# A hybrid-attention and mixture-of-experts encoder block on one core: early loads dealt to two queues, one warm-up pair of products less, and an earlier turn of the second query tile

## The chip, the cores and the metric

The kernel runs on one core of one Trainium2 chip. The metric is the device time of one execution in microseconds (us), with all weights and inputs in the chip's DRAM at the start. Three timed runs of the kernel before gave 576.99, 577.24 and 577.96 us: the median is 577.24 us.

## The reference, cut to what matters

One encoder layer over 256 tokens of width 1024, everything in float32:

```python
n = rms_norm(h, norm1_g)
p = n @ w_in                      # 1024 x 1536: columns [qA | kA | vA | qB | kB | vB]
A = global attention, 8 query heads, 2 key/value heads; q and k are RMS-normalised per head and rotated
B = windowed attention (|i-j| <= 128), 8 heads, sink logit per head, T5 relative-position bias
h = h + concat[rms_norm(A), rms_norm(B)] @ w_o
h = h + hier_moe(rms_norm(h, norm2_g))   # top-1 of 4 groups, then top-2 of its 8 experts
return rms_norm(h, final_g)

# hier_moe: 32 experts, each silu(x @ w_gate) * (x @ w_up) @ w_down
#           w_gate, w_up: 1024 x 512; w_down: 512 x 1024 (2 MB each, so 6 MB an expert)
```

The 32 experts have 201 MB of weights; all of them are read once.

## The kernel before

All of it is one program written engine by engine, with semaphores between the engines: SyncE (`sp`) issues nearly all loads in a fixed order, ScalarE (`act`) issues a few, TensorE (`pe`), VectorE (`dve`) and GpSimd (`pool`) compute. Each engine works through its own list in the order in which it is written, and a wait stops everything behind it on that engine. Tokens are two tiles of 128 (t = 0, 1).

**Start (lines 300 to 320, 483 to 500, 656 to 661, 1011 to 1052).** SyncE loads the gains `gT` (12 KB), then in turn the four pieces of the transposed input `xT` (256 KB each, two column chunks a piece) and the eight chunks of `w_in` (768 KB each), the input itself (`h`, two halves) after chunk 5, and two tables of constants. ScalarE at the same time issues seven small loads: `onehot` (32 partitions of 2 KB), `relb` (32 partitions of 32 bytes), and five that spread a row over 128 partitions (`qn_g`, `kn_g`, `sink`, `b_group`, `b_expert`). TensorE multiplies zeros twice (`multiply_zeros(2)`, two products of 128x128 by 128x512, each of which shows as two passes), waits for `onehot` and `relb`, makes with them one product of 32x8 by 32x512, the line of the relative-position bias (line 1018), and multiplies zeros twice more. VectorE scales each chunk of `xT` by `gT`. Then TensorE projects: for each of the 8 chunks c it waits for the scaled `xT` chunk and for `w_in` chunk c and makes three products (line 1032); after these come eight products more that need nothing new. ScalarE copies the bias line out of PSUM (line 493), GpSimd masks it, ScalarE stores it to DRAM and, once `w_in` chunk 5 has landed, reads it back in shifted rows (`bias_in`), after which SyncE goes on with `w_o` and the experts' weights.

**Attention (lines 1055 to 1160).** Eight steps s = 0 to 7, each of four heads: `scores`, the row maxima (`maxima`, VectorE), the exponentials (`exps`, ScalarE), `turn_probs` (transposes), the cut of these (`cut_probs`, one half on VectorE, one on ScalarE) and `weigh_v`. Steps 0 to 3 are the windowed group, 4 to 7 the global one. In between VectorE rotates the global queries of each tile (`rotate(t)`, with GpSimd's help for the norm), TensorE turns them (`turn(ps[7], pair_cols(t, ...))`) and VectorE copies them (`turn_out`), which steps 4, 5 (tile 0) and 6, 7 (tile 1) need. Scores of step s + 2 are issued at the end of step s. Also in between TensorE projects the mixed heads by `w_o` (`project`, line 1101, bank 7), and VectorE adds that to `h` (`add_projection`, line 727).

**Experts (from line 1201).** A ring of 11 slots of 2 MB holds weights. `sp` issues the load of fill f once fill f - 11 has been used (`wait_used`). Units 0 to 3 have 2 experts, the seven behind them 4; a unit gathers its tokens, multiplies by gate and up (line 1240), by down (line 1255), and scatters (line 1277).

Of the kernel before, what the change touches and what calls it, by code (L numbers as in the profile page):

```python
# [116 lines left out]
def build_encoder(nc, x, x_cols, gain_cols, norm1_g, w_in, qn_g, kn_g, sink, rel_bias, gnorm_a, gnorm_b, w_o, norm2_g,  # L117
# [10 lines left out]
    with ExitStack() as ctx:  # L128
# [171 lines left out]

        @block.sync
        def _(sp):
            sp.dma_start(gT[:], gain_cols).then_inc(gain_in, 16)
            for c in range(KC):
                if c < 4:
                    sp.dma_start(xT[:, 2 * c:2 * c + 2, :], x_cols[:, 2 * c:2 * c + 2, :]).then_inc(xT_in[c], 16)
                sp.dma_start(w_in_sb[:, c, :], w_in_c[c]).then_inc(w_in_in[c], 16)
                if c == 5:
                    for t, arrived in enumerate((x_in, x1_in)):
                        sp.dma_start(h[:, t, :], x_t[t]).then_inc(arrived, 16)  # L310
            sp.dma_start(cst[:], consts).then_inc(consts_in, 16)
# [168 lines left out]

        @block.scalar
        def _(act):
            act.dma_start(onehot_sb, onehot).then_inc(onehot_in, 16)
            act.dma_start(relb_sb, rel_bias).then_inc(onehot_in, 16)
            act.dma_start(gains[:, 0, :], qn_g[0].partition_broadcast(P)).then_inc(small_in, 16)
            act.dma_start(gains[:, 1, :], kn_g[0].partition_broadcast(P)).then_inc(small_in, 16)
            act.dma_start(sink_b[:], sink[0].partition_broadcast(P)).then_inc(router_in, 16)
            act.dma_start(router_b[:, 0:4], b_group[0].partition_broadcast(P)).then_inc(router_in, 16)
            act.dma_start(router_b[:, 4:36], b_expert[0].partition_broadcast(P)).then_inc(router_in, 16)


            act.wait_ge(line_ready, 1)
            act.activation(line_sb, ps[7][0:8, :], ACT.Copy).then_inc(line_cut, 1)
            act.wait_ge(line_masked, 1)
            act.dma_start(bias_line, line_sb).then_inc(line_stored, 16)
            act.wait_ge(line_stored, 16)
            act.wait_ge(w_in_in[5], 16)
            shifted = bass.AP(bias_line.tensor, 0, [[1, P], [4 * P, 8], [1, 3 * P]])
# [148 lines left out]
        def _(dve):  # L647
# [68 lines left out]
            def mix_out(g, t, k, bank=7):  # L716

                dve.wait_ge(mix_turned, k)
                dve.tensor_tensor(mixT[:, 1 - g, t], ps[bank][:].rearrange("p (c t) -> p c t", c=4),
                                  bcast(gT[:, 8 + 4 * g:12 + 4 * g], 2, P), ALU.mult).then_inc(mixT_ready, 1)  # L720
# [29 lines left out]
                dve.tensor_tensor(qt_, qt_, bcast(rq[t], 2, HD), ALU.mult).then_inc(roped, 1)  # L750

            for s in range(8):
                if s != 3:
                    maxima(s)
                if s >= 1:
                    cut_probs(s - 1)
                if s == 0:
                    dve.wait_ge(qk_turned, 4)
                    dve.tensor_copy(qkT[:, 4, :], ps[5][:, 256:512]).then_inc(qkT_ready, 1)
                if s == 2:  # L760
                    maxima(3)
                    dve.wait_ge(qkv_done, 4)
                if s >= 2:
                    outputs(s - 2)
                if s == 1:
                    rotate(0)
                if s == 2:
                    turn_out(5, 0)
                if s == 3:
                    mix_out(1, 0, 1)  # L770
                    rotate(1)
                if s == 4:
                    dve.wait_ge(ro_ready, 1)
                    add_projection(1, 0, 0, 1, 7)
                    turn_out(6, 1)
                if s == 5:
                    add_projection(1, 0, 1, 2, 7)
                if s == 6:
                    mix_out(1, 1, 2)
                if s == 7:  # L780
                    dve.wait_ge(ro_ready, 2)
                    add_projection(1, 1, 0, 3, 7)

                    dve.wait_ge(router_w_in, 32)
                    dve.tensor_tensor(router_w, router_w, bcast(gT[:, 16:24], 2, 36), ALU.mult).then_inc(router_ready, 1)
# [224 lines left out]
        def _(pe):  # L1010
            def multiply_zeros(n):
                for _ in range(n):
                    pe.matmul(ps[6][:], zeros[:, 0:P], zeros[:, P:P + 512], start=True, stop=True)  # L1013
# [2 lines left out]
            multiply_zeros(2)  # L1016
            pe.wait_ge(onehot_in, 32)
            pe.matmul(ps[7][0:8, :], relb_sb, onehot_sb, start=True, stop=True).then_inc(line_ready, 1)
            multiply_zeros(2)

            def turn(dst, srcs, done):

                for k, src in enumerate(srcs):
                    last = pe.transpose(dst[:, k * P:k * P + src.shape[0]], src, ident[0:src.shape[0], 0:src.shape[0]])
                last.then_inc(done, 1)
# [69 lines left out]
            def turn_mix(g, t, bank):  # L1095
                pe.wait_ge(o_ready, 4 * (1 - g) + 2 * t + 2)
                turn(ps[bank], [o_sb[:, t, 512 * g + c * P:512 * g + (c + 1) * P] for c in range(4)], mix_turned)
# [21 lines left out]
            for s in range(8):  # L1119
# [4 lines left out]
                    turn(ps[7], [pair_cols(0, b) for b in range(0, 4)], qk_turned)  # L1124
                if s == 3:
                    turn_mix(1, 0, 7)
                if s >= 1:
                    weigh_v(s - 1)
                if s == 2:
                    pe.wait_ge(qkT_ready, 5)  # L1130
                if s == 4:
                    pe.wait_ge(roped, 2)
                    pe.wait_ge(h_added, 1)
                    turn(ps[7], [pair_cols(1, b) for b in range(0, 4)], qk_turned)
                    pe.wait_ge(qkT_ready, 6)
                if s + 2 < 8:
                    scores(s + 2)
# [253 lines left out]
```

## Time and profile before

| | |
|---|---|
| Median of three runs | 577.24 us (576.99 to 577.96) |
| Profiled execution, whole | 579.82 us |
| Its span, first to last instruction | 578.0 us |
| TensorE busy | 442.7 us (77%) |
| VectorE / ScalarE / GpSimd busy | 115.7 / 63.3 / 28.2 us |
| Moved by DMA | 218.72 MB, mean 378 GB/s over the span |
| Chain of waits: TensorE / DMA | 51% / 42% of the span |

The rows of all views are times from the start of the span. The profiled execution is 579.82 us against a span of 578.0 us, 1.8 us lie around it, and it is 2.6 us over the median of the timed runs.

### The profile page before, as it was taken

To read this page: it belongs to the slowest core of one execution; us is meant where nothing else is said; L and a number is where in the kernel's file an instruction comes from. 1 tells how busy PE (TensorE), PEld (TensorE's weight loads), DVE (VectorE), ACT (ScalarE), POOL (GpSimd) and SP (SyncE) were. 2 spreads that over 40 slices of the span, in tenths; PEclk is the share of its full clock that TensorE was granted. 3 is DMA by queue.
4 is the path that set the end of the run, shared out by engine and by line. 5 is a ranking of instruction groups with operands and counts; after the bars stand their busy time and mean duration, and the time that the engine had idled before them with its cause. 6 is when DMAs were issued, how large, how long until landed. Compare 5 with 4: busy or idle time off the path is not lost.

```text
span 578.0 us, 6194 instructions
## 1 busy us (share of the span) xinstructions
PE 442.7 (77%) x2544; PEld 200.1 (35%) x2544; DVE 115.7 (20%) x282; ACT 63.3 (11%) x127; POOL 28.2 (5%) x58
## 2 busy tenths in 40 slices
PE   8999989989999999999247726673658254837665
PEld 3446767564435353525012401240114011412111
DVE  1007664252204040404001200030004000300204
ACT  1114232222000000000000000000000000000002
POOL 0052200040000000000000000000000000000001
PEclk9999999999999999999687877788869786986797
DMA  7989980855989999999999999999999999999982
GB/s 281 403 322 430 427 332 0 328 182 175 387 356 429 417 430 425 429 427 424 430 430 425 429 427 430 427 424 427 433 424 429 425 429 431 426 426 429 418 340 75
DMA packets 24190, 218.72 MB, mean 378 GB/s; under 512 B 5176, under 2 KB 6456, under 8 KB 12128
## 3 DMA queue, kind: packets, MB, share of 16 engines
q1 hardware_dynamic: 19920, 215.36, 89.3%
q10 hardware_dynamic: 4240, 2.94, 1.7%
q8 instruction: 21, 0.34, 0.2%
q14 instruction: 9, 0.07, 0.0%
HBM read 217.23 MB, written 1.06 MB: 378 GB/s over the span
## 4 chain that ended last, share of the span: by engine, by line
PE 51%; DMA 42%; DVE 2%; SPq 2%; POOL 2%; issue 1%; ACT 0%; POOLq 0%; DVEq 0%; ACTq 0%
PE bank L1240 20%; DMA ring<-in_w_gate_dram 15%; DMA ring<-in_w_down_dram 14%; DMA ring<-in_w_up_dram 11%; PE bank L1255 8%; PE bank L1032 7%; PE bank L1211 3%; PE bank L1277 3%; PE bank L1091 2%; DMA g2b<-in_norm_g_dram 2%; PE bank L1101 2%; SPq L378 2%; PE bank L1080 1%; PE bank L1013 1%; PE bank L1069 1%
## 5 line engine op out<-in xcount | busy, mean ns | idle before, releaser
L1240 PE MATMUL bank<-ring,region_x 128*32 128x512 f32 (+1 forms) x1024 | 161.0, 681 | 106.2 <-DMA ring<-in_w_gate_dram 58.3
L1240 PEld LDWEIGHTS bank<-ring,region_x 128*32 128x32 f32 (+1 forms) x1024 | 47.4, 130 | 217.6 <-issue 217.6
L1255 PE MATMUL bank<-ring,region_q 128*32 128x512 f32 (+1 forms) x512 | 76.2, 637 | 15.3 <-DMA ring<-in_w_down_dram 14.5
L900 DVE TENSOR_TENSOR region_q<-region_q,bank 128x512 f32<-128x512 f32 x10 | 6.9, 688 | 293.2 <-PE bank L1240 293.2
L1255 PEld LDWEIGHTS bank<-ring,region_q 128*32 128x32 f32 (+1 forms) x512 | 23.2, 122 | 60.6 <-issue 54.0
L1032 PE MATMUL bank<-ring,region_x 128*128 128x512 f32 x96 | 42.2, 594 | 0.0
L1277 PE MATMUL bank<-region_x,region_q 128*128 128x512 f32 x80 | 39.0, 621 | 0.0
L1211 PE MATMUL bank<-region_q,region_t 128*128 128x128 f32 x320 | 37.4, 275 | 0.3 <-DVE region_q L879 0.3
L1211 PEld LDWEIGHTS bank<-region_q,region_t 128*128 128x128 f32 x320 | 36.6, 192 | 0.3 <-issue 0.3
L906 DVE TENSOR_TENSOR h<-h,bank 128x512 f32<-128x512 f32 x40 | 27.5, 688 | 42.2 <-PE bank L1277 42.2
L1101 PE MATMUL bank<-ring,region_q 128*128 128x512 f32 x64 | 28.9, 597 | 0.0
L1032 PEld LDWEIGHTS bank<-ring,region_x 128*128 128x128 f32 x96 | 18.1, 191 | 22.2 <-issue 21.7
L608 ACT ACTIVATE region_x<-bank 128x512 f32<-128x512 f32 x10 | 6.0, 597 | 165.5 <-PE bank L1211 165.5
L476 POOL TENSOR_SCALAR stat<-stat 128x1 f32<-128x1 f32 x2 | 0.4, 190 | 447.6 <-ACT region_t L644 447.5
L1277 PEld LDWEIGHTS bank<-region_x,region_q 128*128 128x128 f32 x80 | 12.6, 188 | 27.1 <-DVE h L906 13.1
L614 ACT ACTIVATE region_q<-bank 128x512 f32<-128x512 f32 x10 | 6.0, 597 | 131.9 <-PE bank L1240 131.9
L620 ACT ACTIVATE region_x<-bank 128x512 f32<-128x512 f32 x18 | 10.7, 597 | 84.9 <-PE bank L1255 84.9
L1101 PEld LDWEIGHTS bank<-ring,region_q 128*128 128x128 f32 x64 | 11.6, 190 | 12.6 <-issue 12.6
L1091 PE MATMUL bank<-region_v,ring 128*128 128x65 f32 x128 | 15.2, 272 | 0.0
L1091 PEld LDWEIGHTS bank<-region_v,ring 128*128 128x128 f32 x128 | 15.0, 192 | 0.5 <-issue 0.5
L891 DVE COPY region_x<-bank 128x512 f32<-128x512 f32 x10 | 6.9, 692 | 24.0 <-PE bank L1211 24.0
L727 DVE SCALAR_TENSOR_TENSOR h<-bank,stat,h 128x512 f32<-128x512 f32 x8 | 6.0, 750 | 19.0 <-PE bank L1101 16.2
(183 smaller groups left out, 244.5 us busy)
## 6 DMA issues: line engine op xcount, KB each, us to landing
ring<-in_w_up_dram SPq DMA_DIRECT2D x32, 2048.0 KB, 31.2
ring<-in_w_gate_dram SPq DMA_DIRECT2D x31, 2048.0 KB, 29.4
ring<-in_w_down_dram SPq DMA_DIRECT2D x27, 2048.0 KB, 30.7
ring<-in_w_in_dram SPq DMA_DIRECT2D x8, 768.0 KB, 12.2
ring<-in_w_down_dram SPq DMA_DIRECT2D x12, 512.0 KB, 18.4
ring<-in_w_o_dram SPq DMA_DIRECT2D x2, 2048.0 KB, 11.6
ring<-in_w_down_dram SPq DMA_DIRECT2D x4, 1024.0 KB, 14.7
ring<-in_w_gate_dram SPq DMA_DIRECT2D x4, 512.0 KB, 8.4
```

The source lines that it names most:

```text
L378: sp.dma_start(slots[fill_slot(fill_at(UNITS - 1, 2, a))][:, cols], down_e[bass.ds(experts[a], 1), :, cols].rearrange("a p d -> (a p) d")) ...
L620: act.activation(y_slots[:, 512 * half:512 * half + 512], ps[GD0 + half][:], ACT.Copy).then_inc(y_ready, 1)
L891: dve.tensor_copy(xgT[:, 4:8, :], ps[GD1][:].rearrange("p (c s) -> p c s", c=4)).then_inc(xg_dve, 1)
L900: dve.tensor_tensor(act_sb, silu_sb, ps[UP][:], ALU.mult).then_inc(act_done, 1)
L906: dve.tensor_tensor(part, part, ps[SC0 + k % 2][:], ALU.add).then_inc(sc_free, 1)
L1032: return pe.matmul(ps[bank][:], xT[:, c, t * P:(t + 1) * P], cols, start=(c == 0), stop=(c == KC - 1))
L1091: last = pe.matmul(ps[6][:, 65 * l:65 * l + 65], probsT[:, s % 2, kt, l, :], v_sb[:, kt, 2 * g + l // 2, :], start=(kt == 0), stop=(kt == ...
L1101: last = pe.matmul(ps[bank][:], mixT[:, 1 - g, t, c - 4 * g, :], w_o_sb[g][:, c - 4 * g, 512 * half:512 * half + 512], start=(c == 4 * g), ...
L1211: last = pe.matmul(ps[GD0 + b][:, c * P:(c + 1) * P], hn[:, t, 4 * b + c, :], pick[:, t, :], start=(t == 0), stop=(t == TT - 1))
L1240: last = pe.matmul(ps[bank][rows, :], xgT[:, c, rows], slots[fill_slot(f + a)][:, c * F:(c + 1) * F], start=(c == 0), stop=(c == KC - 1))
L1255: last = pe.matmul(ps[GD0 + half][rows, :], hT[:, c, rows], slots[fill_slot(f + a)][:, c * D + 512 * half:c * D + 512 * half + 512], start ...
L1277: last = pe.matmul(ps[SC0 + k % 2][:], place_w[:, (k // 2) * P:(k // 2 + 1) * P], y_slots[:, 512 * (k % 2):512 * (k % 2) + 512], start=Tru ...
```

## The change

Five edits:

1. SyncE's list no longer has `gT` and the first piece of `xT`; it begins with `w_in` chunk 0, and each further `xT` piece is issued behind the `w_in` chunk of its number. The two halves of `h` come behind chunk 6 instead of chunk 5.
2. ScalarE's list begins with the first piece of `xT` and `gT`; `onehot` and `relb` follow as third and fourth.
3. The five small spread loads move behind the store of the bias line and behind a new wait for `w_in` chunk 1.
4. TensorE's second `multiply_zeros(2)` is gone.
5. In the attention steps, VectorE's `maxima(4)` moves from step 4 to step 3, ahead of `mix_out` and `rotate(1)`; TensorE's turn of the second query tile moves in step 4 ahead of `weigh_v(3)`.

```diff
         def _(sp):
-            sp.dma_start(gT[:], gain_cols).then_inc(gain_in, 16)
             for c in range(KC):
-                if c < 4:
+                sp.dma_start(w_in_sb[:, c, :], w_in_c[c]).then_inc(w_in_in[c], 16)
+                if 0 < c < 4:
                     sp.dma_start(xT[:, 2 * c:2 * c + 2, :], x_cols[:, 2 * c:2 * c + 2, :]).then_inc(xT_in[c], 16)
-                sp.dma_start(w_in_sb[:, c, :], w_in_c[c]).then_inc(w_in_in[c], 16)
-                if c == 5:
+                if c == 6:
                     for t, arrived in enumerate((x_in, x1_in)):
                         sp.dma_start(h[:, t, :], x_t[t]).then_inc(arrived, 16)
 ...
         def _(act):
+            act.dma_start(xT[:, 0:2, :], x_cols[:, 0:2, :]).then_inc(xT_in[0], 16)
+            act.dma_start(gT[:], gain_cols).then_inc(gain_in, 16)
             act.dma_start(onehot_sb, onehot).then_inc(onehot_in, 16)
             act.dma_start(relb_sb, rel_bias).then_inc(onehot_in, 16)
+
+            act.wait_ge(line_ready, 1)
+            act.activation(line_sb, ps[7][0:8, :], ACT.Copy).then_inc(line_cut, 1)
+            act.wait_ge(line_masked, 1)
+            act.dma_start(bias_line, line_sb).then_inc(line_stored, 16)
+            act.wait_ge(w_in_in[1], 16)
             act.dma_start(gains[:, 0, :], qn_g[0].partition_broadcast(P)).then_inc(small_in, 16)
 ... (kn_g, sink, b_group, b_expert as before)
-            act.wait_ge(line_ready, 1)
-            act.activation(line_sb, ps[7][0:8, :], ACT.Copy).then_inc(line_cut, 1)
-            act.wait_ge(line_masked, 1)
-            act.dma_start(bias_line, line_sb).then_inc(line_stored, 16)
             act.wait_ge(line_stored, 16)
             act.wait_ge(w_in_in[5], 16)
 ...
             for s in range(8):
-                if s != 3:
+                if s not in (3, 4):
                     maxima(s)
 ...
                 if s == 3:
+                    maxima(4)
                     mix_out(1, 0, 1)
                     rotate(1)
 ...
             pe.matmul(ps[7][0:8, :], relb_sb, onehot_sb, start=True, stop=True).then_inc(line_ready, 1)
-            multiply_zeros(2)
 ...
+                if s == 4:
+                    pe.wait_ge(roped, 2)
+                    pe.wait_ge(h_added, 1)
+                    turn(ps[7], [pair_cols(1, b) for b in range(0, 4)], qk_turned)
                 if s >= 1:
                     weigh_v(s - 1)
                 if s == 2:
                     pe.wait_ge(qkT_ready, 5)
                 if s == 4:
-                    pe.wait_ge(roped, 2)
-                    pe.wait_ge(h_added, 1)
-                    turn(ps[7], [pair_cols(1, b) for b in range(0, 4)], qk_turned)
                     pe.wait_ge(qkT_ready, 6)
```

## Rows read from the trace of the kernel before

**Rows 1.** Chain of waits in order of time: start us, us, what.

```profile
10.79 27.47 PE bank L1032 x64
...
103.59 12.11 DMA g2b<-in_norm_g_dram
...
260.94 25.92 DMA ring<-in_w_gate_dram
```

**Rows 2.** Stretches: us, busy of PE, PEld, DVE, ACT, POOL, PEclk, DMA share, GB/s.

```profile
160.00:164.00 4.00, 4.00 (x20) 1.29 (x18) 0.00 (x0) 0.60 (x1) 0.00 (x0) 1.00 0.69 201
164.00:168.00 4.00, 4.00 (x22) 1.36 (x20) 0.00 (x0) 0.60 (x1) 0.00 (x0) 1.00 1.03 442
```

**Rows 3.** Timeline, 0 to 12 us: start, us, engine, line, what [idle before <-releaser].

```profile
2.13 0.45 ACTq L486 DMA_DIRECT2D ring<-in_kn_g_dram  x1
...
5.32 0.10 PEld L1018 LDWEIGHTS bank<-ring 32*8 32x8 f32 x2 [1.53 <-DMA ring<-in_rel_bias_dram]
5.32 1.87 PE L1018 MATMUL bank<-ring 32*8 32x512 f32 x2
...
7.12 3.67 PE L1013 MATMUL bank<-region_t 128*128 128x512 f32 x4
```

**Rows 4.** Timeline, the same stretch: weight loads, one ahead of each pass.

```profile
8.99 0.34 PEld L1013 LDWEIGHTS bank<-region_t 128*128 128x128 f32 x1 [0.52 <-issue]
...
9.84 0.34 PEld L1032 LDWEIGHTS bank<-ring,region_x 128*128 128x128 f32 x1 [0.52 <-issue]
...
10.63 0.19 PEld L1032 LDWEIGHTS bank<-ring,region_x 128*128 128x128 f32 x1 [0.45 <-issue]
...
11.06 0.19 PEld L1032 LDWEIGHTS bank<-ring,region_x 128*128 128x128 f32 x1 [0.24 <-issue]
```

**Rows 5.** DMA issues by target: queue, count, KB each, median us to landing.

```profile
ring<-in_qn_g_dram ACTq DMA_DIRECT2D x1, 32.0 KB, 6.7
ring<-in_kn_g_dram ACTq DMA_DIRECT2D x1, 32.0 KB, 7.9
```

**Rows 6.** The eight loads of `w_in` (line 307): from issue to landing.

```profile
DMA to landing us min/median/max: 7.1/12.2/18.9
```

**Rows 7.** TensorE's weight loads at three later restarts; first slow and first fast one.

```profile
366.17 0.23 PEld L1240 LDWEIGHTS bank<-ring,region_x 128*32 128x32 f32 x8 [10.81 <-issue]
...
369.28 0.14 PEld L1240 LDWEIGHTS bank<-ring,region_x 128*32 128x32 f32 x4 [0.31 <-issue]
...
405.79 0.23 PEld L1240 LDWEIGHTS bank<-ring,region_x 128*32 128x32 f32 x8 [12.02 <-issue]
...
409.99 0.14 PEld L1240 LDWEIGHTS bank<-ring,region_x 128*32 128x32 f32 x4 [0.56 <-issue]
...
523.38 0.23 PEld L1240 LDWEIGHTS bank<-ring,region_x 128*32 128x32 f32 x8 [13.27 <-issue]
...
529.36 0.15 PEld L1240 LDWEIGHTS bank<-ring,region_x 128*32 128x32 f32 x4 [0.63 <-issue]
```

**Rows 8.** Timeline, 64 to 79 us: step 4 and the second query tile.

```profile
64.55 1.14 PE L1069 MATMUL bank<-region_t 64*128 64x256 f32 x8
...
67.18 0.69 DVE L719 TENSOR_TENSOR region_q<-bank,gT 128x512 f32<-128x512 f32 x1 [1.63 <-PE bank L1024]
...
69.87 3.70 PE L1101 MATMUL bank<-ring,region_q 128*128 128x512 f32 x8
...
71.49 0.68 DVE L686 TENSOR_REDUCE stat<-bank 128x2 f32<-128x512 f32 x1
...
72.80 0.17 DVE L688 TENSOR_SCALAR stat<-stat 128x4 f32<-128x4 f32 x1
...
74.29 0.74 DVE L727 SCALAR_TENSOR_TENSOR h<-bank,stat,h 128x512 f32<-128x512 f32 x1
...
74.62 1.14 PE L1080 MATMUL bank<-cst,ring 128*128 128x128 f32 x8 [1.05 <-ACT ring L542]
...
78.73 1.13 PE L1069 MATMUL bank<-region_t 64*128 64x256 f32 x8 [0.78 <-DVE region_t L732]
```

## The prediction, made before the changed kernel ran

> **What bounds the kernel now.** I read the chain of waits in order of time first. From 260.94 us on its long pieces are waits for expert weights, the first of them 25.92 us [rows 1]: the end is set by the stream of weights, which moves the same bytes whatever the change does. So the question is when the stream last ran dry. The stretches say it: up to 160 to 164 us DMA stands at a share of 0.69 and 201 GB/s, in 164 to 168 us at 1.03 and 442 GB/s [rows 2], and no later stretch before the last one of loading drops like that. Until then a load waits for a slot that TensorE frees, and TensorE is the one that is late. Hence the rule for this change: what makes TensorE's list reach 160 us earlier or later moves the whole stream and the end by as much, one for one. It is a list with few holes. From 10.79 us it runs 64 passes of the input projection without a pause [rows 1]; the holes that the change touches are 1.53 us ahead of the bias line [rows 3] and 1.05 and 0.78 us around step 4 of the attention [rows 8]. The 12.11 us wait for a gain vector at 103.59 us [rows 1] is issued behind the last attention output and behind loads that TensorE releases, so it travels with TensorE and is no cushion.
>
> **The attention edit, step 4.** Before, VectorE idles 1.63 us until 67.18 [rows 8], then does the mix copy and the rotation, and only at 71.49 begins the maxima of step 4, which end with the negation at 72.97 (72.80 + 0.17) [rows 8]: 1.48 us. ScalarE's exponentials follow, and TensorE, done with the projection that began at 69.87 and took 3.70 [rows 8], stands still 1.05 us. Step 4's scores end at 65.69 (64.55 + 1.14) [rows 8], so in its new place the maxima run from about 65.7 to 67.2 in that idle time, and the mix copy and rotation begin where they did, at worst 0.1 us later. The exponentials end at some 68.8, long ahead of 73.5: the 1.05 us go. What could be late next is the second query tile's turn, moved ahead of the weighing. It needs the rotation (ends 71.57, after its last instruction) and the addition to `h` that frees bank 7: projection end 73.5 plus 0.74 for that addition [rows 8] is 74.3, while TensorE comes to the turn after eight transposes, at 74.4 to 74.6. So it doesn't wait, by 0.1 to 0.3 us. The copy of the turned tile then lies beside the sixteen products of the weighing (1.7 us against a copy of 0.7), and the 0.78 us go as well. Idle alone is 1.83 us; the two restarts also cost a few tenths of fill time (1.14 us for eight transposes that take about 0.9 in a dense list). Ends 1.7 and 2.2 us; I take **2.0 us gained**. The moved cut of step 3's transposes on VectorE comes earlier than before, at 71.6 instead of 72.88, so nobody waits for it. The router's two loads, which ScalarE issues behind step 4's exponentials, go out some 4 us earlier into a busy stream; they are needed 20 us later.
>
> **The start: what is removed.** The second pair of zero products is 3.67 us at 7.12 [rows 3]. But it doesn't stand there idly. Weight loads come 0.85 us apart up to 9.84 and 0.43 us apart from 10.63 [rows 4]: passes run at the 1.2 GHz pace up to then, at the 2.4 GHz pace after. (The granted clock of the profile says 1.00 from the start here; the pace doesn't.) The first pass of real work is the first quick one. Without the pair the projection itself is what TensorE does while the clock is low. How long that lasts the restarts after long idle show: 3.1, 4.2 and 6.0 us from the first slow to the first quick load [rows 7], and three more lie at 3.4 to 4.4. I take 4.1 us. In it the projection gets through 4.1/0.85 = 4.8 passes that would take 2.06 us at the quick pace, so 2.0 us are lost (1.5 to 3.0 at the ends). It is no less here because there were zeros before: they end at 5.0, and then nothing runs until the bias line. The line product, 32 rows by 8 columns, didn't bring the clock up before either, though TensorE was busy with it for 1.87 us.
>
> **The start: what is moved.** TensorE's list still has the bias line ahead of the projection, and the line needs `relb`. That load was second on ScalarE's queue and landed at 5.3 [rows 3]. Now it is fourth, behind 128 partition rows of `xT`, 128 of `gT` and 32 of `onehot`; with its own 32 that is 320 rows. Nothing in the trace is exactly that, but `kn_g` was at the same depth: `onehot` 32, `relb` 32, `qn_g` 128, itself 128, also 320. It was issued at 2.13 [rows 3], just as `relb` will be, and took 7.9 us [rows 5]: landed 10.0. `qn_g`, 128 rows less deep, landed 1.6 us ahead of it (issued at 1.66, 6.7 us [rows 5]). These loads have 32 KB each, so it isn't their bytes that take the time, and the other queue's large rows are what lay beside them. Low end: `relb` lands as long after its issue as now, 2.13 + 4.1 = 6.2. High end: ahead of it or beside it lie now two chunks of `w_in` and a piece of `xT`, 1.8 MB; of the loads before, the third piece of `xT` had 2.4 MB up to and with it and landed at 12.3, the second 1.3 MB and 9.5, so some 11.5. I take 10.0.
>
> The Trainium skill bears on this. Its page "DMA: Bandwidth & Descriptors", section "Queues, rings and completion order", says that each DMA engine takes turns between the queues that have work for it; and section "Issuing engines are not separate DMA queues" that a second issuing engine saves issue time only. By the first, what is put ahead of `relb` in its own queue counts, as `kn_g` shows here. By the second, two queues bring the bulk no sooner: `relb` would wait for 1.8 MB at the 442 GB/s of the steady stream [rows 2], 4.1 us after a first byte near 2.3, so 6.4, and the time would be the first rival's.
>
> So the line product runs 10.0 to 11.9 and the projection begins at 11.9 instead of 10.63: 1.3 us lost, and the slow pace on top, 2.0 us. The new order of the chunks on SyncE's queue brings `w_in` chunk 0 sooner than the 8.8 of before (issued at 1.66 plus the least of 7.1 [rows 6]), which helps nobody if TensorE isn't there until 11.9. Chunk 7 landed at about 27.5 (the last issue at 8.6, the most 18.9 [rows 6]) and is now needed at 31 to 32. The two halves of `h` land about 2 us later, near 24 and 26; the norm's chain behind them takes 4 us and was needed at 31.5, now later. The five spread loads land after 14 us; the first to need them waits anyway for the table that lands at 29.95. ScalarE's new wait for chunk 1 has behind it these loads, the readback of the bias and the squares; chunk 5, for which the readback waits, lands at 20.6, so the new wait costs nothing. **3.3 us lost at the start**, ends +0.4 (line at 6.2, so the start set by `w_in` chunk 0 at 8.7; slow pace of 3.1 us) and -5.5.
>
> **The sum.** 3.3 lost, 2.0 gained: 1.3 us lost. In the profiled execution's terms 579.82 becomes 581.1; against the median of the runs, 577.24 + 1.3 = 578.5 us. What a measurement tells from no change here is 0.2%, 1.15 us: faster is under 576.1, slower over 578.4.
>
> **The rivals.**
> 1. `relb` comes soon after its issue, 6.2 to 7 us. Then the line ends at 8.1 to 8.9, the projection begins at 8.7 to 9, 1.8 us before its time, which the slow pace eats (2.0): start even, and step 4 brings the time down to 577.24 + 0.2 - 2.0 = 575.4. For it: `onehot` and `relb` themselves landed in 2.0 and 4.1 us, and large first rows may fill the engines better. Against: five small loads on this queue that landed 1.1 to 1.7 us after each other. It decides once `relb` lands before about 8.5. If the clock besides comes up at once, the start gains 2 us and the time is 573.3; nothing in the trace is like that. Chance 0.25, the last variant 0.03 of it.
> 2. Step 4 brings nothing: the turn waits for the addition to `h`, and weighing, scores and all behind them with it; the 0.1 us of room is gone if the maxima hold the rotation up. The price is up to the 2.0 us: 577.24 + 3.3 = 580.5. Against: two separate holes would both have to be refilled. Chance 0.08.
> 3. The start is worse on both counts, `relb` at 11.5 and a low clock for 6 us: 2.8 + 3.0 lost, less 2.0: 581.0. Chance 0.07.
>
> **How the numbers follow.** The forecast has 0.60, with a range of its own of 577.0 to 580.0 (`relb` at 8.8 to 11, slow pace 3.1 to 5 us); a bit over half of it lies over 578.4. Slower: 0.32 + 0.08 + 0.07 = 0.47. Within: 0.27 and 0.04 of the first rival, 0.31. Faster: 0.22. The range of 8 in 10 goes from 575.0, into the first rival, to 580.5.
>
> **What would show it.** The line product (line 1018) starts near 10.0 with some 5 us of idle before it for `relb`; weight loads of line 1032 begin at 11.5 to 12 and come 0.85 us apart for 3 to 6 us; scores of step 0 start about 3.3 us later than 42.28. From the projection at step 3 to the scores of step 6 it is 6.9 us instead of 8.86 (78.73 - 69.87 [rows 8]), with no hole over 0.2 us. The stretch in which the stream fills for good moves by about +1.3 us. A line product before 8.5, or quick weight loads from the first, would prove the start's sum wrong; a TensorE wait for line 727 or 732 in step 4, the other's.

## The result, and the profile after

The changed kernel is slower. Ten runs of it have a median of 581.02 us (579.32 to 582.66), ten of the kernel before, the three known ahead of the prediction among them, 578.18 us (576.99 to 580.43). The ratio is 1.0044, 95% interval 1.0029 to 1.0059: 2.5 us lost (1.7 to 3.4). The forecast was 578.5 us, that is 1.3 us lost, with a range up to 580.5. The sign was right, the loss is about twice as large, and the time lies outside the range.

The profiled execution took 579.88 us, its span is 578.0 us, the same as the one before. So the two pages show none of the loss: one must follow the places of the change, not the spans. In these two executions the start costs 2.7 us and step 4 gives 1.9 back; the rest of the difference is in a wait that the change doesn't touch, shown at the end of this section. The chain of waits at the start (start us, us, what):

```profile
2.14 7.82 DMA ring<-in_rel_bias_dram
9.96 0.04 issue
10.01 1.87 PE bank L1020 x2
11.88 29.07 PE bank L1033 x64
```

`relb` lands 7.8 us after its issue, the line product runs 10.01 to 11.88, and the 64 passes end at 40.95, not at 38.26 [rows 1]. The timeline of the same stretch, TensorE's passes and weight loads and VectorE's first scaling (start, us, engine, line, what [idle before <-releaser]):

```profile
9.35 0.62 DVE L662 TENSOR_SCALAR region_x<-region_x,gT 128x256 f32<-128x256 f32 x2 [7.82 <-DMA gT<-in_gain_cols_dram]
...
10.01 1.87 PE L1020 MATMUL bank<-ring 32*8 32x512 f32 x2 [5.04 <-DMA ring<-in_rel_bias_dram]
...
13.67 0.34 PEld L1033 LDWEIGHTS bank<-ring,region_x 128*128 128x128 f32 x1 [0.52 <-issue]
...
14.53 0.26 PEld L1033 LDWEIGHTS bank<-ring,region_x 128*128 128x128 f32 x1 [0.52 <-issue]
...
15.03 0.19 PEld L1033 LDWEIGHTS bank<-ring,region_x 128*128 128x128 f32 x1 [0.24 <-issue]
...
15.46 0.19 PEld L1033 LDWEIGHTS bank<-ring,region_x 128*128 128x128 f32 x1 [0.24 <-issue]
```

Weight loads come 0.85 us apart until 14.53 and 0.43 us apart from 15.03: the projection itself runs at the 1.2 GHz pace for 3.1 us, where zeros ran before [rows 4]. The gains landed at 9.3 us, 8.2 us after their issue; before, they landed 2.2 us after it and nothing waited for them. Step 4:

```profile
68.42 0.69 DVE L687 TENSOR_REDUCE stat<-bank 128x2 f32<-128x512 f32 x1 [0.18 <-PE bank L1070]
...
69.87 0.69 DVE L720 TENSOR_TENSOR region_q<-bank,gT 128x512 f32<-128x512 f32 x1
...
72.56 3.70 PE L1102 MATMUL bank<-ring,region_q 128*128 128x512 f32 x8
...
76.10 1.04 PE L1081 MATMUL bank<-cst,ring 128*128 128x128 f32 x8
...
77.27 0.63 PE L1025 MATMUL bank<-cst,region_q 128*128 128x128 f32 x4
...
79.56 1.13 PE L1070 MATMUL bank<-region_t 64*128 64x256 f32 x8
```

From projection to scores it is 79.56 - 72.56 = 7.00 us, 8.86 before [rows 8], and neither hole is left: 1.86 us gained. The two stretches of [rows 2] again:

```profile
160.00:164.00 4.00, 4.00 (x22) 1.35 (x20) 0.00 (x0) 0.60 (x1) 0.00 (x0) 1.00 0.62 176
164.00:168.00 4.00, 4.00 (x22) 1.38 (x20) 0.00 (x0) 0.41 (x1) 0.00 (x0) 1.00 1.01 434
```

From the end of the 64 passes to the first product of the gathers it is 87.26 us after and 89.65 us before, 2.39 us less, of which step 4 has 1.86. The other half microsecond is one wait of TensorE for VectorE at the router, which the profiled execution of before has at 1.39 us and four further executions of it at 0.84 or 0.85, as after. First the line of before, then that of after:

```profile
126.12 0.41 PE L1196 MATMUL bank<-region_q,cst 128*128 128x32 f32 x2 [1.39 <-DVE region_q L855]
```

```profile
126.42 0.41 PE L1198 MATMUL bank<-region_q,cst 128*128 128x32 f32 x2 [0.84 <-DVE region_q L857]
```

### The profile page after: what moved, and what is told of

Its sections match the earlier page's. It is cut to its first block, busy times and chain, and to the rows that moved or that the text cites. A ratio compares the mean times of both kernels' runs of the same rounds, so it can differ in the third digit from the quotient of the medians.

```text
span 578.0 us, 6186 instructions
## 1 busy us (share of the span) xinstructions
PE 438.1 (76%) x2540; PEld 199.3 (34%) x2540; DVE 116.0 (20%) x282; ACT 63.4 (11%) x127; POOL 28.2 (5%) x58
## 4 chain that ended last, share of the span: by engine, by line
PE 54%; DMA 41%; SPq 2%; DVE 1%; issue 1%; ACTq 0%; POOLq 0%; DVEq 0%; ACT 0%; POOL 0%
PE bank L1242 20%; DMA ring<-in_w_gate_dram 15%; DMA ring<-in_w_down_dram 13%; DMA ring<-in_w_up_dram 11%; PE bank L1257 8%; PE bank L1033 7%; PE bank L1102 5%; PE bank L1213 3%; PE bank L1279 3%; PE bank L1092 2%; SPq L377 2%; PE bank L1070 1%; DMA ring<-in_rel_bias_dram 1%; PE bank L1025 1%; PE bank L1081 1%
## 5 line engine op out<-in xcount | busy, mean ns | idle before, releaser
L1257 PE MATMUL bank<-ring,region_q 128*32 128x512 f32 (+1 forms) x512 | 74.1, 619 | 13.5 <-DMA ring<-in_w_down_dram 12.7
L1033 PE MATMUL bank<-ring,region_x 128*128 128x512 f32 x96 | 43.7, 612 | 0.0
L1279 PEld LDWEIGHTS bank<-region_x,region_q 128*128 128x128 f32 x80 | 12.9, 191 | 27.3 <-DVE h L908 13.1
L621 ACT ACTIVATE region_x<-bank 128x512 f32<-128x512 f32 x18 | 10.7, 597 | 82.0 <-PE bank L1257 82.0
```

What stands on the lines that cost most here:

```text
L621: act.activation(y_slots[:, 512 * half:512 * half + 512], ps[GD0 + half][:], ACT.Copy).then_inc(y_ready, 1)
L1033: return pe.matmul(ps[bank][:], xT[:, c, t * P:(t + 1) * P], cols, start=(c == 0), stop=(c == KC - 1))
L1257: last = pe.matmul(ps[GD0 + half][rows, :], hT[:, c, rows], slots[fill_slot(f + a)][:, c * D + 512 * half:c * D + 512 * half + 512], start ...
L1279: last = pe.matmul(ps[SC0 + k % 2][:], place_w[:, (k // 2) * P:(k // 2 + 1) * P], y_slots[:, 512 * (k % 2):512 * (k % 2) + 512], start=Tru ...
```

## The experiments

The ratios are against runs of the kernel before on the same chip. Diffs are against the kernel named. In the kernels' own line numbers, lines 1018 to 1020 or 1041 and 1042 are the line product, 1030 to 1033 the projection, 1193 or 1195 four products that only keep TensorE busy ahead of the router ("keepers"), 1211 or 1213 the gathers' products, 1255 or 1257 the products with `w_down`.

**e1_step4_only: before, with the attention edit alone**

```diff
-                if s != 3:
+                if s not in (3, 4):
                     maxima(s)
 ...
                 if s == 3:
+                    maxima(4)
 ... (TensorE's turn of the second tile ahead of weigh_v, as in the change)
```

> The kernel before with the attention edit alone (maxima of step 4 and the second tile's turn moved up). Theory 1, the sum of the prediction with a start that costs more in most executions than in the one profiled: the edit gives 1.9 us, the gap from the step 3 projection to the scores of step 6 falls from 8.86 to 7.0 us and the time from the median of before by 1.9 us (ratio 0.9967). Theory 2, the attention edit's gain is absorbed later (by the load of the gain vector at 104 us or by the stream): the gap still falls, but the time stays within 0.5 us of before, and the edits at the start alone are worth their 2.5 us.

Median 577.02 us (575.63 to 578.46, 12 runs) against 578.19; ratio 0.9982 (0.9965 to 0.9998): 1.0 us gained (0.1 to 2.0). The step takes 7.01 us, as in the changed kernel. The unexpected lines are at the start and at the router, TensorE's timeline:

```profile
5.29 1.03 PE L1019 MATMUL bank<-ring 32*8 32x512 f32 x2
...
6.25 1.98 PE L1014 MATMUL bank<-region_t 128*128 128x512 f32 x4
...
8.58 3.88 PE L1033 MATMUL bank<-ring,region_x 128*128 128x512 f32 x8 [0.35 <-DMA ring<-in_w_in_dram]
...
119.00 6.13 PE L1195 MATMUL bank<-cst 128*128 128x448 f32 x8
```

The start is that of the kernel before, and yet the line product takes 1.03 us and not 1.87 [rows 3], the second zeros 1.98 and not 3.67 [rows 3]: the first zeros took 3.78 us as before, the 2.4 GHz pace was there by the line product, and the 64 passes ended at 37.14 us. The keepers took 6.13 us where the profiles of both kernels have 3.25. So one kernel differs from execution to execution in at least two places.

**e2_start_only: after, without the attention edit**

```diff
-                if s not in (3, 4):
+                if s != 3:
                     maxima(s)
 ... (maxima(4) and the turn back in their old places)
```

> The changed kernel with the attention edit undone: loads on two queues, five small ones later, no second pair of zeros. Theory 1: 2.5 us (what the whole change cost) + 1.9 us given back = 4.4 us slower than before (ratio 1.0076); line product at 10.0 us, projection at 11.9, slow pace 3 to 6 us. Theory 2: 2.5 us slower (1.0043), as with the attention edit.

Median 581.96 us (580.60 to 583.82, 7 runs), ratio 1.0072 (1.0045 to 1.0099): 4.2 us lost (2.6 to 5.7). The line product began at 10.10, the projection at 11.90, quick weight loads came from 15.5, the passes ended at 41.40, 3.1 us behind the profile of before. The start is the whole loss.

**e3_line_loads_first: after, with the line's two loads at the head of ScalarE's queue**

```diff
+            act.dma_start(onehot_sb, onehot).then_inc(onehot_in, 16)
+            act.dma_start(relb_sb, rel_bias).then_inc(onehot_in, 16)
             act.dma_start(xT[:, 0:2, :], x_cols[:, 0:2, :]).then_inc(xT_in[0], 16)
             act.dma_start(gT[:], gain_cols).then_inc(gain_in, 16)
-            act.dma_start(onehot_sb, onehot).then_inc(onehot_in, 16)
-            act.dma_start(relb_sb, rel_bias).then_inc(onehot_in, 16)
```

> The changed kernel with one exchange: the two loads of the bias line (onehot, relb) are again first on ScalarE's queue, ahead of the first piece of xT and gT. Theory 1, the depth in the queue is what delays the line: relb lands near 5.3 us, the line product ends at 7.2, the projection begins when gT and w_in chunk 0 are there, 8.5 to 9.5, at the slow pace for 3 to 6 us: start about even with before (between 0.5 us gained and 1 us lost), time 1 to 2.4 us under before (0.9975), 3.5 to 4.5 us under the changed kernel. Rival, the two queues share so that the line's loads land late in any order once large rows of w_in lead the other queue: line product at 8 us or later, and at most 1 us under the changed kernel.

Median 580.82 us (579.21 to 582.29, 12 runs), ratio 1.0043 (1.0025 to 1.0060). My expectation failed. Its timeline:

```profile
6.24 1.87 PE L1020 MATMUL bank<-ring 32*8 32x512 f32 x2 [0.88 <-DMA ring<-in_rel_bias_dram]
...
11.06 1.85 DVE L662 TENSOR_SCALAR region_x<-region_x,gT 128x256 f32<-128x256 f32 x6 [9.54 <-DMA gT<-in_gain_cols_dram]
...
11.47 2.08 PE L1033 MATMUL bank<-ring,region_x 128*128 128x512 f32 x2 [3.36 <-DVE region_x L662]
```

The line is 3.8 us earlier, but now `gT` is the fourth in the queue: issued at 2.13, landed 8.9 us later, at 11.04. The projection begins 0.4 us earlier than in the changed kernel, no more. It isn't `relb` itself that is slow but what it stands behind on this queue. Whether the fourth place or the 256 KB piece of `xT` ahead makes the load late, this run doesn't separate: `gT` has both here, and in the changed kernel, second and right behind the piece, it took 8.2 us.

**e4_no_second_zeros: before, without the second pair of zero products**

```diff
             pe.matmul(ps[7][0:8, :], relb_sb, onehot_sb, start=True, stop=True).then_inc(line_ready, 1)
-            multiply_zeros(2)
```

> The kernel before without its second pair of zero products, loads untouched. Theory 1, the pair pays for itself by bringing the clock up while TensorE would wait anyway: the projection begins at 8.8 us (landing of w_in chunk 0) instead of 10.6 but at the slow pace for 3 to 6 us, so 1.8 us gained and 1.5 to 3.0 lost: between 0.3 us faster and 1.2 us slower, 0.3 us slower at the middle. Rival, the pair is only a cost: 1.8 us faster (ratio 0.997).

Median 579.43 us (577.68 to 580.53, 12 runs), ratio 1.0015 (0.9998 to 1.0033): 0.9 us lost (-0.1 to 1.9, so no loss is just within the interval, and the rival's gain of 1.8 us is out). The projection waits 1.61 us for `w_in`, begins at 8.79, 2 us before its old time, runs slow until 14.6, and the passes end at 39.24, 1.0 us later than before.

**e5_line_behind_chunk0: before, with the attention edit, five zero products in one block and the line product behind chunk 0**

```diff
-            multiply_zeros(2)
-            pe.wait_ge(onehot_in, 32)
-            pe.matmul(ps[7][0:8, :], relb_sb, onehot_sb, start=True, stop=True).then_inc(line_ready, 1)
-            multiply_zeros(2)
+            multiply_zeros(5)
 ...
                 last = qkv(0, QB, c, 2)
+                if c == 0:
+                    pe.wait_ge(onehot_in, 32)
+                    pe.matmul(ps[7][0:8, :], relb_sb, onehot_sb, start=True, stop=True).then_inc(line_ready, 1)
```

> The kernel before with the attention edit, and at the start five zero products in one block instead of two and two around the bias line, whose product moves behind the three products of chunk 0. Loads as before. Theory 1, before starts its projection by chance of the clock: in the profile of the kernel with the attention edit alone the slow pace ended at about 6 us and the projection began at 8.6, bound by w_in, in the profile of before it ended at 10.6. One dense block of products should end the slow pace before 8.8 us in nearly every execution: projection at 8.6 to 9.2 us at the quick pace, its 64 passes over at 37 to 37.5 us; time 0.3 to 1 us under the attention edit alone (577.0), so 576.4, ratio to before 0.997. Rival, the clock at the start varies little and costs nothing on average: no change from 577.0.

Median 577.0 us (575.65 to 578.61, 12 runs), ratio 0.9978 (0.9964 to 0.9993). The zeros end at 8.7, the projection begins at 8.81 at the quick pace, the line product of 11.56 takes 1.02 us, the passes end at 37.67. The start is as theory 1 has it, the time is not: against the attention edit alone (e1, ratio 0.9982) the gain is 0.2 us, with intervals that overlap almost wholly, where 0.3 to 1 us was expected. The timed runs don't show that a late quick pace at the start costs anything on average, nor do they exclude it.

**e6_h_behind_w_in: e5, with the loads of `h` behind the last chunk of `w_in`**

```diff
-                if c == 5:
+                if c == 7:
```

> As e5, with the two halves of h behind w_in chunk 7 instead of chunk 5. If, with a quick start, the projection waits for the last chunks of w_in (24.9 us in the profile of the attention edit alone), its 64 passes end at 36.3 instead of 37.2 and the time falls by 0.8 us against e5. Rival: the norm of h, which comes 2.5 us later, holds up the cuts behind the projection (ready at about 30.3 us, needed at 28.8), and nothing is gained or up to 1.5 us lost.

Median 576.72 us (575.06 to 578.29, 12 runs), ratio 0.9965 (0.9946 to 0.9983). It beats both kernels; from e5 it can't be told, and its profile shows no earlier passes (ended at 37.92).

**e7_two_keepers: e5, with two keepers instead of four**

```diff
-            for _ in range(4):
+            for _ in range(2):
                 pe.matmul(ps[0][:, 0:448] ...
```

> As e5, with two of the four products behind the router logits (line 1193 of before: identity by constants) instead of four. Theory: in some executions TensorE's clock falls during the router's small products (0.50 from 118 us in the profile of the attention edit alone, 1.00 in that of before), the four products then take 5.9 us instead of 3.25 and the rank products behind them start at 125.0 instead of 122.6: with two this delay goes, 0 us in executions with a quick clock and 1.5 to 2.4 in those with a slow one, 0.7 us under e5 in the median and a narrower spread. Rival: the clock is then low for the gathers and the first expert products, and the time is over e5's by up to 1.5 us.

Median 578.72 us (576.89 to 581.23, 12 runs), ratio 1.0004 (0.9987 to 1.0022), 1.5 us over e5 by the ratios, whose intervals overlap a little. The gathers' 32 passes took 5.71 us and not 3.81. The rival held: the keepers earn their time. That the loss comes from the gathers' pace is read from this one execution.

**e8_zeros_bridge_wait: after, with five zero products instead of two ahead of the line's wait**

```diff
-            multiply_zeros(2)
+            multiply_zeros(5)
             pe.wait_ge(onehot_in, 32)
```

> The changed kernel with five zero products instead of two ahead of its wait for the bias line's loads, so that TensorE is busy until they land at 10.0 us. Theory 1 (half of what the start costs is the delay of the line, half the slow pace behind it): the line product runs from 10.0 to 10.9 at the quick pace, the projection from 11.0 at the quick pace; 0.9 + 2.0 us under the changed kernel, 578.1 us, ratio to before 1.000. Rival 1, only the delay counts: 0.9 us under the changed kernel at most. Rival 2, the line product lets the clock fall again and nothing is gained.

Median 578.79 us (576.71 to 581.13, 12 runs), ratio 1.0005 (0.9989 to 1.0022), as expected. Its timeline:

```profile
1.58 6.74 PE L1015 MATMUL bank<-region_t 128*128 128x512 f32 x10 [1.58 <-DVE region_t L657]
...
10.06 1.02 PE L1020 MATMUL bank<-ring 32*8 32x512 f32 x2 [1.74 <-DMA ring<-in_rel_bias_dram]
...
11.01 1.55 PE L1033 MATMUL bank<-ring,region_x 128*128 128x512 f32 x3
```

`relb` is as late as ever, but TensorE was busy until 8.3, the line product runs at the quick pace and so does the projection; the passes end at 38.74 instead of 40.95, 2.2 us earlier. That is what the slow pace takes here: 1.4 us of projection and 0.9 of line product, and the ratio fell by as much (0.0039, 2.3 us). Only the 1.4 are a cost of the change: the line product is slow in the profiled execution of before too [rows 3].

**e9_after_line_behind_chunk0: after, with the arrangement of e5**

```diff
-            multiply_zeros(2)
-            pe.wait_ge(onehot_in, 32)
-            pe.matmul(ps[7][0:8, :], relb_sb, onehot_sb, start=True, stop=True).then_inc(line_ready, 1)
+            multiply_zeros(5)
 ... (the line product behind chunk 0, as in e5)
```

> The kernel after with its loads as they are, five zero products in one block and the line product behind chunk 0 of the projection. Theory (the change's order of loads only loses, by the late line and by gT): the line's table of 10.0 us no longer holds TensorE up, but the gains land at 9.3 us and the first scaled piece follows at about 9.7, so the projection begins at 9.8 us, 1.0 us behind the same arrangement with the loads of before (8.81); the line product stands at about 12.4, the 64 passes end near 38.5 (37.67 there), the time is 577.9 us, ratio 0.999. Rival (the line alone was the fault, and the dealt loads bring the first chunks sooner): projection at 8.8 us or earlier, passes ended by 37.5, ratio 0.996 or lower.

Median 578.15 us (576.57 to 581.14, 12 runs), ratio 0.9996 (0.9979 to 1.0012). Its chain:

```profile
1.17 8.20 DMA gT<-in_gain_cols_dram
...
9.40 0.36 DVE region_x L662
...
9.81 2.84 PE bank L1031 x6
12.65 0.95 PE bank L1042 x2
13.60 25.09 PE bank L1031 x58
```

The theory said 9.8: `gT` holds the projection until 9.81, 1.0 us behind e5 with the same TensorE list, and the passes end at 38.69 against 37.67. So the dealt loads have no gain of their own that the late line hid; they cost 1.0 us even where nothing waits for `relb`.

**Further profiled executions of the two kernels and of e5**

> The kernel before again, for a second profile of the same program. Theory (chance of the clock at the start): the end of the slow pace differs from one execution to the next, between about 4.5 and 10.5 us; where it ends by 8 us the projection begins at 8.6 to 9 us (w_in bounds it) and its 64 passes end at 37.1 to 37.7 instead of 38.3. Rival: every profile of this program shows the slow pace up to 10.4 to 10.6 us and the 64 passes ending at 38.2 to 38.4.

> A third profile of the kernel before, with the same two expectations as the second.

> The changed kernel again, for a second profile. Theory: here the slow pace always starts with the projection at 11.9 us, and it ends between 14.9 and 18 us, 14.9 having been the kindest case: 64 passes end at 40.9 to 42.4 us. Rival: the end is at 40.9 again.

> A third profile of the changed kernel, with the same two expectations as its second.

> The kernel before once more, a look at its start and its router. Two theories on why the change cost 2.5 us in the timed runs and not the 1.3 us worked out from one execution. Theory A: the profiled execution of before was one in which the clock came up late (quick weight loads from 10.6 us); in others it comes up at 6 to 7 us and the 64 passes end at 37.1 instead of 38.3 to 38.5. Then about every second look shows the early rise. Theory B: the start always ends at 38.2 to 38.5 and the difference comes from the router's clock.

> The kernel after once more. Theory A: quick weight loads from 15.0 us at the earliest and 17 us at the latest, 64 passes ended at 41 to 42 us, never the early rise of before, since TensorE stands from 5.0 to 10 us. Theory B (the router's clock): the gathers' products (line 1213) take 5 us instead of 3.8 in most executions.

> As the look before it of the kernel before: by theory A an end of the 64 passes at 37.1 or at 38.3 to 38.5 us, by theory B always the later one and quick or slow products at the router to tell the executions apart.

> The kernel of the line product behind chunk 0 and five zero products once more. Its twelve executions spread from 575.65 to 578.61 us, though its start should be the same in each. Theory A (the start's clock is settled by the five products): the 64 passes end at 37.6 to 37.8 us again, and an execution over 576.8 us shows its difference at the router: keepers of 5 to 6 us, or gathers' products of 5.1 to 5.6 us instead of 3.8. Theory B: the start varies here too, with quick weight loads from 10 us or later and passes ended at 39 us.

> As the look before it: by theory A passes ended at 37.6 to 37.8 us whatever the time, and the router's products tell the executions apart; by theory B a late end of the passes in the slower execution.

All in one table, read from the chains and timelines; us from the start of the span. In the last column slow means that 14.3 to 14.6 us lie between the last weights and the end of the span, quick 12.8 to 12.9:

| execution | time | first quick weight load | 64 passes end | gathers' products: start, us | last weights land | the last 16 down products |
|---|---|---|---|---|---|---|
| before, profiled | 579.82 | 10.6 | 38.26 | 127.91, 3.81 | 563.50 | slow |
| b_look1 | 578.15 | 6.8 | 37.12 | 126.23, 3.81 | 561.75 | slow |
| b_look2 | 579.86 | 10.9 | 38.51 | 127.63, 3.81 | 563.51 | slow |
| b_look3 | 580.02 | 10.7 | 38.32 | 127.43, 3.81 | 563.64 | slow |
| b_look4 | 580.15 | 10.8 | 38.43 | 127.54, 3.81 | 563.75 | slow |
| after, profiled | 579.88 | 15.0 | 40.95 | 128.21, 3.81 | 563.57 | slow |
| a_look1 | 582.60 | 16.8 | 41.86 | 129.12, 5.44 | 566.48 | slow |
| a_look2 | 580.01 | 15.4 | 41.32 | 128.58, 3.81 | 563.74 | slow |
| a_look3 | 581.07 | 16.9 | 41.97 | 129.24, 5.43 | 566.41 | quick |
| e5, profiled | 575.65 | 6.9 | 37.67 | 124.93, 3.81 | 560.93 | quick |
| e5_look1 | 577.31 | 4.9 | 37.63 | 124.89, 3.81 | 560.89 | slow |
| e5_look2 | 575.93 | 6.7 | 37.80 | 125.64, 3.81 | 561.29 | quick |

Three places are at the quick pace in some executions of one kernel and at the slow one in others; I call each outcome a draw. The first is the start, and only where the zero products leave it open: in before it was late in four of five, where theory A expected about every second one early. This is b_look1, the early one, on TensorE:

```profile
5.30 1.05 PE L1018 MATMUL bank<-ring 32*8 32x512 f32 x2
...
6.28 1.98 PE L1013 MATMUL bank<-region_t 128*128 128x512 f32 x4
...
8.57 3.85 PE L1032 MATMUL bank<-ring,region_x 128*128 128x512 f32 x8 [0.31 <-DMA ring<-in_w_in_dram]
```

and the chain of b_look2, a late one:

```profile
5.76 1.87 PE bank L1018 x2
7.63 3.41 PE bank L1013 x4
11.04 27.47 PE bank L1032 x64
```

The second is the router. In a_look3 the stretch of its gathers had a granted clock of 0.65 (a stretch of which a part runs at 1.2 GHz), in the profiled execution of after 1.00, and the same 32 passes took 5.43 and 3.81 us. First the line of the changed kernel's profile, then that of a_look3:

```profile
128.21 3.81 PE L1213 MATMUL bank<-region_q,region_t 128*128 128x128 f32 x32 [0.28 <-DVE region_q L881]
```

```profile
129.24 5.43 PE L1213 MATMUL bank<-region_q,region_t 128*128 128x128 f32 x32 [0.28 <-DVE region_q L881]
```

The third is the last expert, after the last weights have landed. The profile of e5, then e5_look1, both on TensorE:

```profile
560.97 1.92 PE L1257 MATMUL bank<-ring,region_q 128*32 128x512 f32 x16 [2.58 <-DMA ring<-in_w_down_dram]
```

```profile
560.93 3.59 PE L1257 MATMUL bank<-ring,region_q 128*32 128x512 f32 x16 [3.03 <-DMA ring<-in_w_down_dram]
```

In the stretch from 561 to 564 us the granted clock is 1.00 in the first and 0.50 in the second. The last weights land at 560.93 and 560.89 us, and the two times differ by 1.66 us: it is all in these 16 passes (3.59 - 1.92 = 1.67). So for e5 my theory A was right on the start and wrong on the router: what told the two groups apart there was the end, which neither theory had named. In e5_look2 the keepers took 4.95 us and the gathers came 0.7 us later, of which 0.36 was left when the last weights landed.

## Why the prediction was right in its parts and wrong in its number

**The late line: right.** `relb` landed 7.8 to 8.0 us after its issue in all four executions, at 9.93 to 10.10 us; taken from `kn_g`'s row [rows 5]: 10.0. Rival 1 is out. The 6.4 us that the prediction worked out behind the Trainium skill, page "DMA: Bandwidth & Descriptors", section "Issuing engines are not separate DMA queues", did not come either. What the traces show is that the fourth load on this queue is late in three orders: `kn_g` (7.9), `relb` (7.8) and `gT` (8.9 in e3). That a count of rows ahead sets it is not shown: by that count `gT`, with 256 rows up to and with it, should land sooner after its issue than `kn_g` with 320, and took 8.2 us. So part of the hit on 10.0 may be luck. What I overlooked is that `gT`, second in it, is late too: 8.2 us. I charged the change for one load of two, and e9 shows that the second would have cost 1.0 us by itself. It stood in the shade of the first, so the sum wasn't touched. The 1.53 us that the prediction calls a hole ahead of the bias line [rows 3] are idle time of the weight loads only; the zero passes themselves run from 1.58 for 3.78 us, up to the line product, and not to 5.0. No term rested on that either.

**The slow pace on the projection: right.** I took 4.1 us from the projection's first pass. In the four executions of after it lasted 3.2, 5.0, 3.5 and 4.9 us (11.8 to 15.0, 11.8 to 16.8, 11.9 to 15.4, 12.0 to 16.9), mean 4.2. e8 shows the cause: with the wait filled by zeros the pace is quick and the passes end 2.2 us earlier, by the profile and by the ratio alike. In e4, without the late line, the same 64 passes took 30.45 us instead of 27.47.

**The start's sum: right, late executions against late ones.** The passes ended at 41.53 us in the mean of four executions of after, at 38.38 in the mean of the four late ones of before: 3.15 us against 3.3 predicted. (The bad end of this sum, -5.5, should read -5.8, the 2.8 + 3.0 of rival 3. The 581.0 of rival 3 is close to what was measured, but by chance: its conditions, `relb` at 11.5 and a slow pace of 6 us, came in none of the four executions.)

**Step 4: right in the profile.** 1.86 us against 2.0, without a wait for the rotation or the addition; the maxima begin 0.18 us after the scores, in the idle time as described. Rival 2 is out. In time e1 gives 1.0 us (0.1 to 2.0), and e2 against the changed kernel 1.6 by the ratios, whose intervals overlap.

**The step that failed: "against the median of the runs, 577.24 + 1.3".** In the profiled execution's own terms the forecast was 579.82 + 1.3 = 581.1, and the changed kernel's median is 581.02; but that agreement is luck, since its own profiled execution took 579.88. The offset of 2.6 us between the profiled execution and the median, which I took over unchanged, isn't a constant of the profiler: the profiled executions of e3 and e5 are the fastest of their twelve runs. The draws above account for some of it, and one outcome of them, the early start, was not seen in the changed kernel. Two parts:

- The base. The three runs shown all lie in the lower of two groups that the kernel before has: of its 30 runs beside e1, 15 lie at 576.5 to 578.0 and 15 at 578.4 to 581.2. (The 35 beside e5 show no such gap, so take "groups" with care; three low draws are plain enough.) Ten runs have 578.18, which is 0.94 us of my miss of 2.5.
- The change. The term of 1.3 us measured 2.5 (1.7 to 3.4). The early start, 1.1 to 1.4 us in the passes' end, is open to the kernel before, whose TensorE is busy from 1.58 on but for a hole of at most 0.4 us ahead of the line product. The changed kernel stands still from 5.0 or 5.4 to 10.0 us, and its first quick weight load came at 15.0 at the earliest. Counting all five executions of before, the passes' end differs by 3.4 us, and less 1.86 that is 1.5. To this the router adds: its gathers were slow in two of four executions of after (1.6 us each), in none of five of before. The last weights land at 565.05 in the mean of after and 563.23 in that of before, 1.8 us later; the timed runs say 2.5 (1.7 to 3.4). The rule that the stream moves one for one with TensorE holds to about half a microsecond: from the start of the gathers to the last weights it is 435.5 to 436.2 us in before, and 435.2 to 435.7 in after once the 1.6 us of the slow gathers are taken off.

That the size between 1.5 and 2.5 us comes from the router is argued from nine executions, not shown: e1, e2, e5_look2 and e9 drew slow passes there as well, so it may be chance. That the early start is what the change loses in the timed runs isn't shown either: e5, which had a quick start in three of three executions, gained only 0.2 us over e1. What decides it stays open. That the upper group of before is the late start and the slow end together is an inference too: one early start gave 578.15, and e5's two ends differ by 1.66 us.

On such draws the Trainium skill, page "TensorE: Matmul & The Clock Gate", section "What's actually happening", says that the same kernel counts a different number of slow matmuls from run to run. The trace agrees: quick weight loads from 6.8 or 10.6 to 10.9 us in five executions of one kernel. I had read the restarts of [rows 7] as a spread of a cost, and not asked which of the spread's values the profiled execution of before had drawn.

## What to carry to other kernels

A forecast made on one profiled execution holds against executions with the same draws: look first where the granted clock or the pace could have gone otherwise, and ask whether the change keeps both outcomes open. When small loads share a queue with large ones, work out the landing of each of them by its place, not only of the one that is waited for today: moving `relb` to the front only handed its place to `gT`. And where TensorE must wait at the start, try filling the wait with full-size products: three more ahead of the wait gave back 2.3 us here (e8).

## What the runs showed of the chip that I had not expected

- The same line product, 32 rows by 8 columns with two passes, took 1.87 us or 1.02 to 1.05 us; the kernel before has both, 1.87 and 1.05.
- Five zero products from 1.58 us on settled the start in each of seven executions (three of e5, one each of e6 to e9): quick weight loads came at 4.8 to 6.9 us, always ahead of the real work, though the moment itself varied by 2 us.
- In e8 TensorE stood still for 1.7 us, from 8.3 to 10.06, and went on at the quick pace; after the five or so idle us of the changed kernel it went on at the slow one.
- The granted clock on record for the first microseconds doesn't follow the pace. The same stretches of the changed kernel's profile and, in the second fence, of a_look3, both with weight loads 0.85 us apart (the columns of [rows 2]; the clock is the third number from the end):

```profile
8.00:12.00 4.00, 1.99 (x3) 0.29 (x4) 1.23 (x4) 0.09 (x1) 0.00 (x0) 0.50 1.05 386
12.00:16.00 4.00, 4.00 (x7) 1.73 (x8) 1.34 (x4) 0.50 (x1) 0.34 (x2) 0.67 1.03 415
```

```profile
8.00:12.00 4.00, 1.85 (x3) 0.15 (x3) 1.23 (x4) 0.00 (x0) 0.00 (x0) 1.00 1.04 383
12.00:16.00 4.00, 4.00 (x6) 1.79 (x6) 1.31 (x4) 0.59 (x1) 0.49 (x2) 1.00 1.02 411
```

  In the first the two zero products ahead (four passes) took 3.38 us, so the quick pace had come in their last, and the record shows its fall to 0.50. In the second they took 3.78, all slow, and the record says 1.00 over a pace of 1.2 GHz. At the start only the distance of the weight loads tells the pace.
